# First chunk taken unit by unit, couplings' transposes moved behind a tile of chunk 1, last gate units by halves

## The reference

```python
h = x
for i in range(DEPTH):                                  # DEPTH = 2
    h = h + 0.5 * swiglu(rmsnorm(h, ffn1_norm[i]), ffn1_w_gate[i], ffn1_w_up[i], ffn1_w_down[i])
    z = rmsnorm(h, mix_norm[i]) @ w_in[i]
    # z_b, z_c, z_v, z_s: four parts of z
    y_a = short_conv_group(z_b, z_c, z_v, conv_w[i], conv_b[i])
    y_s = s5_group(z_s, A, B, C, D, log_dt, glu_w, glu_b)   # state scan, then a gated unit
    h = h + concat[rmsnorm(y_a), rmsnorm(y_s)] @ w_out[i]
    h = h + 0.5 * swiglu(rmsnorm(h, ffn2_norm[i]), ffn2_w_gate[i], ffn2_w_up[i], ffn2_w_down[i])
    h = h + (p[i] @ ple_w_proj[i]) * sigmoid(rmsnorm(h, ple_norm[i]) @ ple_w_gate[i])
return rmsnorm(h, final_norm)
# swiglu(u, g, w, d) = (silu(u @ g) * (u @ w)) @ d, with 2816 hidden columns
```

## Time and profile before

| | |
|---|---|
| median of three runs | 1087.4 us (1085.93 to 1090.62) |
| the profiled execution | 1091.05 us |
| its span | 1089.2 us |
| TensorE, matmuls | 1050.0 us, 96% |
| VectorE | 675.1 us, 62% |
| ScalarE | 513.1 us, 47% |
| GpSimd | 408.0 us, 37% |
| granted TensorE clock, mean | 0.973 |

### The profile page before, as it was taken

How to read it: one execution, slowest core, us unless ns; L and a number is a source line. 1 busy time by engine, 2 the same in 40 slices (tenths; PEclk the granted TensorE clock), 3 DMA queues, 4 the chain that set the end, 5 groups by cost and what they waited for, 6 DMA issues and landing times.

```text
span 1089.2 us, 15176 instructions
## 1 busy us (share of the span) xinstructions
PE 1050.0 (96%) x5353; PEld 897.4 (82%) x5353; DVE 675.1 (62%) x772; ACT 513.1 (47%) x696; POOL 408.0 (37%) x605
## 2 busy tenths in 40 slices
PE   6999999999979999999999999999997999999996
PEld 5888888899877888888878888889997888888885
DVE  4555666468976555764777555546698765545464
ACT  4544444473364444444564444435535544444453
POOL 5888999314415888970029300001071100000000
PEclk9999999988989999999999999999798999999998
DMA  9655555241335955555536555552323465555541
GB/s 271 209 181 190 193 193 181 90 158 75 116 103 171 259 191 171 189 195 190 187 123 212 195 180 186 192 192 77 117 78 104 149 211 193 193 190 184 185 156 39
DMA packets 143385, 181.55 MB, mean 167 GB/s; under 512 B 18352, under 2 KB 125552, under 8 KB 143344
## 3 DMA queue, kind: packets, MB, share of 16 engines
q1 hardware_dynamic: 143200, 180.48, 50.3%
q10 hardware_dynamic: 144, 0.52, 0.1%
HBM read 179.93 MB, written 1.05 MB: 166 GB/s over the span
## 4 chain that ended last, share of the span: by engine, by line
PE 84%; DVE 11%; ACT 2%; issue 1%; SPq 1%; DMA 0%; POOL 0%; POOLq 0%; DVEq 0%; ACTq 0%
PE ps L1333 26%; PE ps L1335 26%; PE ps L1334 25%; DVE wL L706 2%; PE ps L1435 2%; PE ps L1345 1%; PE ps L1574 1%; PE ps L1575 1%; DVE regT L848 1%; ACT bufB L550 1%; DVE regT L835 1%; DVE bufA L871 1%; DVE regE L843 1%; PE ps L1451 1%; DVE uL L854 1%
## 5 line engine op out<-in xcount | busy, mean ns | idle before, releaser
L706 DVE TENSOR_TENSOR wL<-raw,wH 128x1024 fp32r<-128x1024 f32 x336 | 429.3, 1320 | 137.8 <-ACT wH L396 137.4
L396 ACT ACTIVATE wH<-raw 128x1024 fp32r<-128x1024 f32 x336 | 335.4, 1051 | 169.1 <-PE ps L1335 161.7
L1333 PE MATMUL ps<-wH,uH 128*128 128x512 f32 x832 | 330.2, 397 | 3.0 <-DVE uL L733 1.6
L1335 PE MATMUL ps<-wH,uL 128*128 128x512 f32 x832 | 324.6, 390 | 0.0
L1334 PE MATMUL ps<-wL,uH 128*128 128x512 f32 x832 | 324.4, 390 | 0.0
L1333 PEld LDWEIGHTS ps<-wH,uH 128*128 128x128 f32 x832 | 156.5, 188 | 36.0 <-DVE uL L733 3.6
L1335 PEld LDWEIGHTS ps<-wH,uL 128*128 128x128 f32 x832 | 156.3, 188 | 33.2
L1334 PEld LDWEIGHTS ps<-wL,uH 128*128 128x128 f32 x832 | 156.6, 188 | 30.8
L1068 POOL TENSOR_SCALAR ms<-ssq 128x2 f32<-128x2 f32 x8 | 4.5, 566 | 439.2 <-ACT bufB L410 409.7
L1333 PE MATMUL ps<-wH,hTH 128*128 128x512 f32 x352 | 140.1, 398 | 0.0
L1335 PE MATMUL ps<-wH,hTL 128*128 128x512 f32 x352 | 137.6, 391 | 0.0
(11 more groups left out here) (172 smaller groups left out, 1232.1 us busy)
## 6 DMA issues: line engine op xcount, KB each, us to landing
raw<-in_ffn_w_down_dram SPq DMA_DIRECT2D x88, 512.0 KB, 3.9
raw<-in_ffn_w_gate_dram SPq DMA_DIRECT2D x87, 512.0 KB, 4.0
raw<-in_ffn_w_up_dram SPq DMA_DIRECT2D x87, 512.0 KB, 5.0
raw<-in_w_in_dram SPq DMA_DIRECT2D x32, 512.0 KB, 4.3
raw<-in_w_out_dram SPq DMA_DIRECT2D x16, 512.0 KB, 4.0
raw<-in_ple_w_gate_dram SPq DMA_DIRECT2D x16, 512.0 KB, 3.7
raw<-in_glu_w_dram SPq DMA_DIRECT2D x4, 512.0 KB, 3.6
raw<-in_ple_w_proj_dram SPq DMA_DIRECT2D x4, 512.0 KB, 3.8
```

The source lines that it names most:

```text
L396: nc.scalar.activation(wH[:, slot, w], raw[:, slot, w], ACT.Copy).then_inc(wh_done, 1)
L706: nc.vector.tensor_tensor(wL[:, slot, w], raw[:, slot, w], wH[:, slot, w].bitcast(F32), ALU.subtract).then_inc((wl_half, wl_done)[a], 1)
L1333: mul(o, sH, vH, start=start, stop=False)
L1335: return mul(o, sL, vH, start=False, stop=stop)
```

## The change

- **First chunk.** In layer 1 it is taken unit by unit (`very_first_gate_up`): unit 0 for tile 0 and then tile 1, unit 1 likewise. The norm's quarters go in the order 0, 2, 1, 3 (`norm_turn` gives each its place), ScalarE splits unit 1 behind all of them, and unit 2 behind the inverse root's wait.
- **Loads.** x's tile 1 is issued by SyncE behind unit 0. The couplings' loads move behind unit 4. TensorE waits for x's loads themselves.
- **GpSimd** clears one table first, counts both tiles as ready, clears two, and spreads the steps after the first inverse root.
- **Vectors.** They are turned behind tile 0 of chunk 1's first unit and copied behind unit 3's split.
- **Couplings' transposes**, in both layers. All three groups go to banks of their own (2, 3, 7) behind tile 0 of chunk 1's second unit, and ScalarE copies them behind `hidden_H` of chunk 0, ahead of the splits of step 1, which is written out ahead of the loop.
- **The end.** Tile 1 of the last gate units is finished by halves (`last_half`). ScalarE and VectorE take the quarters in another order. The mean's factor goes into the squares' scale, so that GpSimd has one step fewer behind the last of them, and ScalarE issues the stores of its halves itself.

The diff, cut to its core. Left out are the same renames in `gained`, `rest` and `norm_H` (`turn` for `q` in the counts and buffers of the norm), the new banks in the copies, and the calls that are moved away from SyncE's stores and the two `finish` calls at the old places.

```diff
 SIDE_BANKS = (0, 1, 6, 7)
+TURNED = (2, 3, 7)
...
         FFN_BASE = (U_FFN1, U_FFN2)
+        def norm_turn(l, m, q):
+            return (0, 2, 1, 3)[q] if l + m == 0 else q
...
-            def ffn(l, base, wg, wu, wd, then=None, later=None):
+            def ffn(l, base, wg, wu, wd, then=None, later=None, after=None):
...
                     unit(l, base + part, slot, halves)
+                    if l == 0 and base + part == 0:
+                        sp.dma_start(xres[:, 1, :], x[0, P:2 * P, :]).then_inc(x_ld[1], 16)
                 chunk(1, (0,))
...
                 back(1)
+                if after:
+                    after()
                 first = 2
...
                 ffn(l, U_FFN1, at(ffn1_w_gate, l), at(ffn1_w_up, l), at(ffn1_w_down, l),
-                    (lambda: (vectors(0), couplings(0))) if l == 0 else None)
+                    (lambda: vectors(0)) if l == 0 else None, None, (lambda: couplings(0)) if l == 0 else None)
                 for j in range(8):
...
                                      xres[:, q // 2, (q % 2) * 512:(q % 2) * 512 + 512].rearrange("p (i n) -> p i n", i=2),
-                                     ACT.Square, accum_out=ssqf[:, q:q + 1]).then_inc(ssq_done, 1)
+                                     ACT.Square, scale=1.0 / 32, accum_out=ssqf[:, q:q + 1]).then_inc(ssq_done, 1)
...
-                silus(l, f, 0, base + 1, between)
-                if f == 0:
-                    c_turned(l, 0)
-                    c_turned(l, 1)
-                    p_turned(l)
-                elif l + 1 < DEPTH:
+                if l + f == 0:
+                    split_at(0, 2)
+                    silus(0, 0, 0, 1)
+                    split_at(0, 3)
+                    vectors_turned(0, KD)
+                else:
+                    silus(l, f, 0, base + 1, between)
+                if f == 1 and l + 1 < DEPTH:
                     vectors_turned(l + 1, 0)
-                with act.Fori(1, NFC) as i:
+                def step(i):
                     hidden_H(l, f, i - 1)
+                    if f == 0 and isinstance(i, int):
+                        c_turned(l, 0)
+                        c_turned(l, 1)
+                        p_turned(l)
                     for part in range(3):
...
                         split(l, i * 3 + u, u % SLOTS, i + (u // SLOTS + 1))
+                step(1)
+                with act.Fori(2, NFC) as i:
+                    step(i)
                 last_hidden_H(l, f)
...
                         act.wait_ge(acc_t0, l * 5 + 5)
-                    if q == 2:
+                    if q == 2 and l + 1 == DEPTH:
+                        act.wait_ge(last_half, 1)
+                    elif q >= 2:
                         act.wait_ge(wt_used, used(l, U_GATE + 3))
...
                 else:
+                    gate(2)
                     last_squares(0)
                     last_squares(1)
-                    gate(2)
                     gate(3)
+                    finish(0)
                     last_squares(2)
                     last_squares(3)
+                    finish(1)
...
                 split_at(0, 0)
+                squares(0, 0, 0)
+                norm_H(0, 0, 2)
                 norm_H(0, 0, 1)
+                norm_H(0, 0, 3)
                 split_at(0, 1)
-                vectors_turned(0, KD)
-                squares(0, 0, 0)
                 squares(0, 0, 1)
-                norm_H(0, 0, 2)
-                norm_H(0, 0, 3)
...
                 nc.scalar.activation(pp[:, t, 0:512], pp[:, t, 0:512], ACT.Copy, scale=rs[:, t:t + 1]).then_inc(fin_act, 1)
+                act.wait_ge(fin_act, t + 1)
+                act.dma_start(out[0, t * P:(t + 1) * P, 0:512], pp[:, t, 0:512]).then_inc(stored, 16)
...
-                hidden(l, f, 0, between)
-                if f == 0:
+                if l + f == 0:
+                    split_at(0, 2)
+                    hidden(0, 0, 0)
+                    split_at(0, 3)
+                else:
+                    hidden(l, f, 0, between)
+                def params_L():
                     dve.wait_ge(pth_done, l + 1)
-                    nc.vector.tensor_tensor(pTL[:], ps[:, 7, :].rearrange("p (k n) -> p k n", k=2),
+                    nc.vector.tensor_tensor(pTL[:], ps[:, TURNED[2], :].rearrange("p (k n) -> p k n", k=2),
                                             pTH[:].bitcast(F32), ALU.subtract).then_inc(ptl_done, 1)
-                with dve.Fori(1, NFC) as i:
+                def step(i):
                     hidden_L(l, f, i - 1)
+                    if f == 0 and isinstance(i, int):
+                        params_L()
                     for part in range(3):
...
                         split(l, i * 3 + u, u % SLOTS)
+                step(1)
+                with dve.Fori(2, NFC) as i:
+                    step(i)
                 for t in range(NT):
...
                 else:
-                    for t in range(NT):
-                        for q in range(2 * t, 2 * t + 2):
-                            gated(q)
-                            added(q)
-                        weighted(t)
-            def weighted(t):
-                if t == 0:
+                    for q in range(3):
+                        gated(q)
+                        added(q)
+                    weighted(0)
+                    weighted(1)
+                    gated(3)
+                    added(3)
+                    finish(0)
+                    weighted(2)
+                    weighted(3)
+                    finish(1)
+            def weighted(q):
+                if q == 0:
                     dve.wait_ge(fin_ld, 16)
-                for q in range(2 * t, 2 * t + 2):
-                    at = slice(512 * (q % 2), 512 * (q % 2) + 512)
-                    dve.wait_ge(x_ready, DEPTH * 16 + 16 + q + 1)
-                    nc.vector.tensor_tensor(pp[:, t, at], xres[:, t, at], regT[:, at], ALU.mult).then_inc(fin_x, 1)
+                t, at = q // 2, slice(512 * (q % 2), 512 * (q % 2) + 512)
+                dve.wait_ge(x_ready, DEPTH * 16 + 16 + q + 1)
+                nc.vector.tensor_tensor(pp[:, t, at], xres[:, t, at], regT[:, at], ALU.mult).then_inc(fin_x, 1)
...
                 half_split(0, 0, 0, 0)
+                half_split(0, 0, 0, 1)
+                gained(0, 0, 2)
                 gained(0, 0, 1)
-                half_split(0, 0, 0, 1)
+                rest(0, 0, 2)
                 rest(0, 0, 1)
-                split_at(0, 1)
-                half_norm(0, 0, 1)
+                gained(0, 0, 3)
+                half_split(0, 1, 1, 0)
+                rest(0, 0, 3)
+                half_split(0, 1, 1, 1)
...
+            clear_tables(regE)
             for t in range(NT):
...
                 pool.sem_inc(x_ready, (18, 2)[t])
-                if t == 0:
-                    clear_tables(regE, Gr)
-                    spread_steps(0)
-            pool.wait_ge(pv_full, 1)
-            clear_tables(Gi, taps)
+            clear_tables(Gr, Gi)
             for l in range(DEPTH):
...
                 if l == 0:
+                    clear_tables(taps)
+                    spread_steps(0)
                     setup_E(l)
...
             for t in range(NT):
+                pool.wait_ge(ssq_done, 8 * DEPTH + (2 * t + 1))
+                link(g.tensor_scalar(ms[:, t:t + 1], ssqf[:, 2 * t:2 * t + 1], 1.0, EPS, ALU.mult, ALU.add))
                 pool.wait_ge(ssq_done, 8 * DEPTH + (2 * t + 2))
-                link(g.tensor_tensor(ms[:, t:t + 1], ssqf[:, 2 * t:2 * t + 1], ssqf[:, 2 * t + 1:2 * t + 2], ALU.add))
-                link(g.tensor_scalar(ms[:, t:t + 1], ms[:, t:t + 1], 1.0 / D, EPS, ALU.mult, ALU.add))
+                link(g.tensor_tensor(ms[:, t:t + 1], ms[:, t:t + 1], ssqf[:, 2 * t + 1:2 * t + 2], ALU.add))
                 g.tensor_tensor(rs[:, t:t + 1], ms[:, t:t + 1], mhalf[:, 0:1], ALU.pow).then_inc(rs_done, 1)
...
                 t, h = q // 2, q % 2
-                pe.wait_ge(x_ready, l * 16 + (16 + 4 * m + q + 1))
+                if l + m == 0:
+                    pe.wait_ge(x_ld[t], 16)
+                else:
+                    pe.wait_ge(x_ready, l * 16 + (16 + 4 * m + q + 1))
                 for k in range(4):
...
                             turn_x(l, 2 * f, 3)
-                            if l == 0 and f == 0:
-                                pe.wait_ge(pvt0_done, 1)
-                                turn_vectors(0)
+            def very_first_gate_up():
+                for part in range(2):
+                    for t in range(NT):
+                        pe.wait_ge(ul_done, 2 * part + t + 1)
+                        if t == 0:
+                            pe.wait_ge(wl_half, part + 1)
+                        gate_up_tile(part, part, t, (lambda n=part: take(0, n)) if t == 0 else None)
+                        if part == 0 and t == 0:
+                            turn_x(0, 0, 2)
+                            turn_x(0, 0, 3)
...
```

(44 more changed lines are left out.)

37 lines of the change are left out of this document (14 added, 23 removed).

## The result

The changed kernel took 1093.9 us (median of seven runs, 1093.7 to 1094.1 apart from one disturbed run of 1130.6, which is left out, as are one of 5753.8 in e5 and one of 2098.3 in e8); the kernel before took 1089.5 beside it (1085.9 to 1091.6). The ratio is 1.0050, 95% interval 1.0028 to 1.0072. Forecast were 1089.1 and a range up to 1092.5, so the time is above the range, and the ratio sits on the bound of 0.5% where 0.90 had been put on "within".

A forecast was written before the change was run, and what follows sets the result against it. TensorE, busy for 96% of the span, was taken as the bound. Start −1.9, its clock +1.6, layer 2's wait +2.1, its clock +1.6, end −1.65 gave +1.75: 1091.05 to 1092.8, less 3.65 for the median, 1089.1; range 1084.5 to 1092.5.

The forecast's parts named there:

- the last of the sum: Whole kernel: from profiled execution to median, 3.65 us lower, so 1092.8 becomes 1089.1.
- The start, −1.9: Layer 1 up to its first down projection: that starts 1.9 us earlier, despite a new wait ahead of it.
- The new waits, 2.0 and 2.1: Ahead of each layer's first down projection: TensorE waits for its weights' split, 2.0 us in layer 1, 2.1 in layer 2.
- The bound of 2.7: Layer 2's new wait: up to 2.7 us if VectorE's two halves run at 1.5 beside GpSimd's tables.
- The clock, 1.6 each: Behind each of the two new waits: a lower TensorE clock costs 1.6 us, zero as the other bound.
- Rival (a): One of the two new waits costs no clock: 1087.5 us; chance 0.27.
- rival (b): Neither new wait costs clock, as the skill page has it: 1085.9 us; chance 0.15.
- The end, −1.65: From the last matmuls to the last store: 1.65 us gained, between 1.2 and 2.0.
- Edits costed at nothing: Loop step written out, new banks, table clearing, waits for x's loads, vectors' load: no cost counted.
- (d): Couplings' loads land late; at 3.7 us after their first transpose was due, 1092.8, slower by 0.5%; chance 0.06.
- (e): Start gains nothing as x's tile 1 lands after 12.14; if 1.9 us late, 1091.0; chance 0.07.
- (c): New waits ahead of the down projections don't come; start gives 4.07 us, layer 2 nothing: 1081.7; chance 0.05.

The follow-up runs named there:

- e5: The changed kernel once more, unaltered, beside the kernel before on another chip: 1094.0 us, ratio 1.0044.
- e8: Kernel before with only layer 2's couplings' transposes and copies moved as in the change: 1092.6 us, ratio 1.0035.
- e4: The kernel before once more, unaltered, as the kernel under test: 1086.2 us, ratio 0.9991.
- e10: e1 plus six thrown-away matmuls in TensorE's 1.42 us wait ahead of the mixer's 64-column matmuls, both layers: 1075.6 us, ratio 0.9879.
- e12: Kernel before plus six thrown-away matmuls in the wait ahead of the mixer's 64-column matmuls, both layers: 1080.6 us, ratio 0.9931.
- e13: Changed kernel plus six thrown-away matmuls in the wait ahead of the mixer's 64-column matmuls, both layers: 1083.6 us, ratio 0.9945.
- e14: e10 plus thrown-away matmuls, 12 ahead of the last input projection unit and 18 ahead of the GLU's, both layers: 1074.6 us, ratio 0.9877.
- e7: e1 plus 23 thrown-away matmuls per layer behind an output projection unit, where TensorE had no wait: 1089.5 us, ratio 1.0015.
- e2: Changed kernel with couplings' copies and parameters' rest behind unit 4's split in layer 2 alone: 1088.8 us, ratio 1.0004.
- e1: Changed kernel with couplings' copies and parameters' rest moved behind unit 4's split in both layers: 1084.3 us, ratio 0.9958.
- e9: Changed kernel with couplings' copies behind unit 4's split in layer 1 alone: 1089.1 us, ratio 0.9997.
- e11: Changed kernel plus nine thrown-away 128-column matmuls ahead of each layer's first down projection: 1083.2 us, ratio 0.9965.
- e3: Changed kernel plus 14 thrown-away 128-column matmuls ahead of each layer's first down projection: 1090.6 us, ratio 1.0007.
- e6: Kernel before with only the change's edits of the end: 1085.4 us, ratio 0.9989.

## Why the prediction missed

**The step that failed** is the last of the sum: "the median of the runs shown is 1087.4, 3.65 lower, so 1092.8 becomes 1089.1." It takes the 3.65 for something that both kernels have. It was the distance between two clock levels of the kernel before. e4 shows the levels side by side (eight runs near 1086 with a clock of 0.978, four near 1090 with 0.972 to 0.977), e5 that the changed kernel has the upper one alone (1092.2 to 1094.2). Three shown runs of 1085.93, 1087.4 and 1090.62 said that the times of the kernel before spread; I didn't read that as a level that a change can take away. The sum against the like execution, 1092.8, lies 0.9 below the measured 1093.7.

**Why the changed kernel has no lower level** is shown in part. That the levels are made in the mixer's 64-column stage is shown by the profiles, and that the idle 1.42 us ahead of it are needed for the slow stretch by the fillings: of the 24 runs of e10, e12, e13 and e14 each is faster than the fastest run of the same kernel with this wait unfilled (1079.6, 1085.0 and 1092.2). The idle time alone is not enough, by e7.

That layer 1's new wait keeps the lower level away is shown by counts. The kernels with that wait unfilled, and the mixer's too, had it in 0 of 28 runs (change 16, e2 12). Those without it or with it filled had a lower level in about half: e1 4 of 12, e9 5 of 12, e11 8 of 12, e3 5 of 12, e6 7 of 12, e8 6 of 11, e7 9 of 12 on two lower levels, the kernel before 59 of 104. e9 differs from the changed kernel by that wait alone; with equal odds in both, 5 of 12 against 0 of 16 would come about once in 100. How idle time near 39 acts on the clock near 240 no run here shows, nor how matmuls elsewhere (e7) take layer 2's stretch away; both stay open.

**The start, −1.9.** It gave −1.08. Unit by unit it went as rebuilt, but chunk 1 began at 25.53 and not 24.95, the couplings' transposes at 34.48 and not 33.8, and the way from there to the first down projection was 6.36 and not 6.0. 0.6 of the miss is the wait ahead of chunk 1, for VectorE's product of tile 0.

**The new waits, 2.0 and 2.1.** 2.13 and 2.18, released by VectorE's wL as written; e1 takes both away by the order alone, e2 and e9 one each, and e8 makes one alone. The bound of 2.7, for VectorE beside GpSimd's tables, did not come.

**The clock, 1.6 each.** 1.70 and 1.70 in the profiled execution, and by e3 it is the idle time that does it. It is no law: e5's and e2's profiles have the gap of layer 1 without a slow stretch, those of e5, e8, e9 and e13 that of layer 2 with one. Rival (a) is thus an outcome among the executions, about 1.5 us below the other (e5's 1092.2 to 1092.7 and 1093.7 to 1094.2); rival (b) is out. The Trainium skill (TensorE: Matmul & The Clock Gate, "Why this matters for your kernels") allows longer gaps than these between bursts of matmuls. This case's trace disagrees: half speed followed the down projections' gaps of 2.13 to 2.19 us in seven of nine cases, and the mixer's of 1.42 us in 19 of 24.

**The end, −1.65.** −1.54 in the profile and 1.4 and 0.9 in the groups of e6. GpSimd's last step is out 3.93 + 0.55 = 4.48 us behind the start of gate(3), where the forecast had 4.47.

**Edits costed at nothing.** No wait for the couplings' loads, for x's second tile or for GpSimd's tables shows in the trace: rivals (d) and (e) did not come, nor (c), which e1 shows was there to be had by one move: 38.71 is 3.2 us ahead of before, where (c) had 4.07.

## What to carry to other kernels

A profiled execution and a median may be of two different clock levels: look whether the times of a kernel fall into groups, lay the granted clock of every run beside its time, find in traces of either group the stretch that differs, and make the sum against an execution of the same level. The mean clock alone doesn't tell the level, as three runs of e5 show. Idle time of TensorE of 1.4 to 2.2 us costs more than itself when half speed follows; where a wait can't be removed, matmuls thrown away into a free bank fill it, six of them in each layer being worth 0.7% of the kernel before and, with the copies behind the weights' split, the change and they together 1.2%. Before filling or speeding a stage, look whether a later wait ends with another engine: what is gained ahead of it is lost there (e14: a mean clock of 0.995 for 0.989, and no time that the ratios could tell).

## What was not expected of the hardware

The clock halved for 14 us in a stage where TensorE was never idle (240 to 248: 2.00 busy of 2.00 us in each window), and this happened only with 1.42 us of idle left ahead of it, though not each time (e7 had the idle time and full clock in both layers). It lost 6.8 us of full speed, four times what followed the 2.2 us gaps of the down projections (1.7). By the times and clocks of e4's runs, in the same kernel on the same chip it fell or did not fall from one execution to the next. A thrown-away matmul of 128 columns in fp32 took 0.218 us in a row of such, where transposes of 128 columns in a row take 0.11.
